# A hybrid encoder layer on one core: rare code moved beside the common code, the last additions shared out anew, one weight load halved

## The reference

```python
h = LN(x) * (1 + scale1) + shift1                 # x: two requests of 256 tokens, 1024 wide
z = h @ w_in + b_in                               # u | v | p | gates
merged = sig(g_a) * (A @ w_branch_a) + sig(g_b) * (P @ w_branch_b)
x = LN(ALPHA * x + gate1 * (merged @ w_out)) * ln1_g + ln1_b
h = LN(x) * (1 + scale2) + shift2
f = moe(h)     # top group of 4, top 2 of its 8 experts; each expert:
               # (silu(xb @ w_gate[e]) * (xb @ w_up[e])) @ w_down[e], width 1024 -> 512 -> 1024
y = LN(ALPHA * x + gate2 * f) * ln2_g + ln2_b
```

## Time and profile before

| | us |
|---|---|
| median of 3 runs | 978.49 |
| lowest, highest | 976.83, 981.91 |
| the profiled execution | 981.18 |
| its span, first to last instruction | 979.5 |
| TensorE busy in it | 912.4 (93%) |
| VectorE, ScalarE, GpSimd busy | 390.6, 242.7, 120.6 |

### The profile page before, as it was taken

How to read it: one execution, slowest core, us unless ns; L and a number is a source line. 1 busy time by engine, 2 the same in 40 slices (tenths; PEclk the granted TensorE clock), 3 DMA queues, 4 the chain that set the end, 5 groups by cost and what they waited for, 6 DMA issues and landing times.

```text
span 979.5 us, 11400 instructions
## 1 busy us (share of the span) xinstructions
PE 912.4 (93%) x4251; PEld 538.5 (55%) x4251; DVE 390.6 (40%) x664; ACT 242.7 (25%) x355; POOL 120.6 (12%) x144
## 2 busy tenths in 40 slices
PE   3789999999999999999999999999896999999973
PEld 1457776888888888786344434444443444344321
DVE  4522344456354236788332223222321222232265
ACT  2422243451234325445411101110110111011114
POOL 2110257000001000000300000000000000000041
PEclk9799999999999999999999999999998999999997
DMA  9884653362224623809899999999999599999953
GB/s 368 334 272 171 251 215 129 128 247 101 87 87 129 194 86 114 272 8 418 323 414 428 425 425 431 425 428 424 429 426 423 220 424 428 425 429 427 422 243 89
DMA packets 44860, 286.92 MB, mean 293 GB/s; under 512 B 5248, under 2 KB 7424, under 8 KB 29170
## 3 DMA queue, kind: packets, MB, share of 16 engines
q1 hardware_dynamic: 37504, 268.18, 67.6%
q0 software_dynamic: 6672, 16.17, 5.5%
q10 hardware_dynamic: 610, 1.66, 0.5%
HBM read 275.84 MB, written 14.58 MB: 297 GB/s over the span
## 4 chain that ended last, share of the span: by engine, by line
PE 83%; DVE 4%; ACT 3%; issue 3%; DMA 2%; SPq 2%; POOLq 0%; POOL 0%; DVEq 0%; ACTq 0%
PE bank L611 81%; DMA modraw<-in_w_mod 2%; PE bank L881 2%; SPq L389 2%; ACT x_rows L1086 2%; DVE total L1970 1%; DVE wo_lo L1650 0%; DVE yout L1858 0%; PE bank L668 0%; POOLq L53 0%; POOL y_out L605 0%; ACT w_hi L1086 0%; PE bank L897 0%; DVE yout L1856 0%; DVE bank L2073 0%
## 5 line engine op out<-in xcount | busy, mean ns | idle before, releaser
L611 PE MATMUL bank<-up_w,x_t 128*64 128x512 f32 x512 | 225.0, 592 | 0.0
L611 PE MATMUL bank<-gate_w,x_t 128*64 128x512 f32 x512 | 225.0, 592 | 0.0
L611 PEld LDWEIGHTS bank<-gate_w,x_t 128*64 128x64 f32 x512 | 70.1, 137 | 143.1 <-issue 143.1
L611 PE MATMUL bank<-h_hi,w_hi 128*128 128x512 f32 x320 | 126.3, 395 | 1.6 <-ACT h_hi L1120 1.6
L611 PE MATMUL bank<-h_hi,w_lo 128*128 128x512 f32 x320 | 125.9, 393 | 0.0
L611 PE MATMUL bank<-h_lo,w_hi 128*128 128x512 f32 x320 | 124.8, 398 | 0.0
L611 PE MATMUL bank<-down_w,hid_t 128*64 128x512 f32 x512 | 118.8, 606 | 6.0 <-issue 5.6
L1319 ACT ACTIVATE sg_hid<-bank 64x512 f32<-64x512 f32 x33 | 19.6, 592 | 348.9 <-PE bank L611 348.9
L1925 DVE TENSOR_TENSOR sg_hid<-bank,sg_hid 64x512 f32<-64x512 f32 x32 | 22.2, 695 | 207.2 <-ACT sg_hid L1319 207.2
L1485 DVE TENSOR_TENSOR w_lo<-raw,w_hi 128x1024 fp32r<-128x1024 f32 x56 | 68.6, 1227 | 78.3 <-ACT w_hi L1086 78.2
L568 POOL DMA_INDIRECT chosen_y<-yout,slot_row x30 | 29.5, 984 | 400.7 <-DVE yout L1943 400.7
(11 more groups left out here) (311 smaller groups left out, 1117.3 us busy)
## 6 DMA issues: line engine op xcount, KB each, us to landing
down_w<-in_w_exp_down SPq DMA_DIRECT2D x32, 2048.0 KB, 17.1
gate_w<-in_w_exp_gate SPq DMA_DIRECT2D x31, 2048.0 KB, 13.6
up_w<-in_w_exp_up SPq DMA_DIRECT2D x31, 2048.0 KB, 18.1
modraw<-in_w_mod SPq DMA_DIRECT2D x24, 1024.0 KB, 8.6
raw<-in_w_in SPq DMA_DIRECT2D x9, 2048.0 KB, 9.9
raw<-in_w_branch_b SPq DMA_DIRECT2D x2, 2048.0 KB, 12.2
chosen_y<-zrow POOLq DMA_DIRECT2D x1, 4096.0 KB, 16.6
raw<-in_w_branch_a SPq DMA_DIRECT2D x2, 2048.0 KB, 10.6
```

Of the source, the lines that this page charges most:

```text
L611: return pe.matmul(out, lhsT, rhs, start=start, stop=stop, skip_group_check=True)
```

## The change

The further code of ScalarE and VectorE is put beside the plain code: `joined_again` is given `with_further(e)` and makes its block before the common continuation. TensorE's stays where it is. At the end the final reads go tile by tile from 0, with a semaphore of its own for the second read of tile 0. VectorE does residual and second choices of tiles 0 and 1 and the residual of tile 2, all ahead of `out_rows(31)`, and gate rows and the first residual ahead of `hidden(31)`. GpSimd adds the second choices of tile 2 after all these, then those of tile 3, to which TensorE adds the residual by a further identity product. Tile 1 is stored through GpSimd's queue, and `gain(1)` comes before `centred_gain(3)`. Expert 3's gate and up weights are loaded in two parts, each of four transfers, the first when the first half of expert 0's gate product is done (`gum_half`); TensorE's wait counts for `e_gu[0]` and `e_half` are raised to match. TensorE has two more products with the identity, of 256 columns, in the router. ScalarE has a silu of one column ahead of its residual copy.

```diff
@@ -184,6 +184,7 @@
         slotw_x = at("slotw_x", [128, 1, 2], f32, V0 + 480)
+        silu_first = at("silu_first", [128, 1], f32, P0 + 64)
         slot_row_x = at("slot_row_x", [128, 1], u32, P0 + 32)
@@ -227,6 +228,7 @@
         s_out = sem("s_out")
+        s_out1 = sem("s_out1")
@@ -304,6 +306,8 @@
         f_g = [sem(f"f_g{i}") for i in range(TILES)]
+        f_second0 = sem("f_second0")
+        gum_half = sem("gum_half")
@@ -328,8 +332,12 @@
-        def joined_again(engine, name):
+        def joined_again(engine, name, further=None):
             engine.br(name + "_on")
+            if further is not None:
+                with nc.body(name + "_further", parent=parted_at[name], valid_engines=[engine.engine]):
+                    further()
+                    engine.br(name + "_on")
             nc.switch_bb(name + "_on", parent=parted_at[name])
@@ -436,7 +444,18 @@
             for e in range(3, NEXP - 2):
-                next_gate_up(e, e % 3)
+                if e == 3:
+                    done = sp.value_load(tab[0:1, 1, 1:2], min_val=0, max_val=16)
+                    for first, freed, loaded in ((0, gum_half, e_half), (2, m_sem["gum"], e_gu[0])):
+                        sp.wait_ge(freed, 1)
+                        sp.sem_inc(sp_go, 1)
+                        sp.wait_ge(x_sem["gum"], done + 1)
+                        sp.sem_inc(sp_go, 1)
+                        for tile, w in ((gate_w[0], w_exp_gate), (up_w[0], w_exp_up)):
+                            for k in (first, first + 4):
+                                sp.dma_start(tile[:, k:k + 2, :], gate_src(w, 3)[:, k:k + 2, :]).then_inc(loaded, 16)
+                else:
+                    next_gate_up(e, e % 3)
                 next_down(e - 1, (e - 1) % 2)
@@ -448,17 +467,17 @@
             sp.sem_inc(sp_go, 1)
-            for i in (2, 3, 0, 1):
-                for j, rows in enumerate((total[i], y_out[i])):
-                    sp.dma_start(rows[:, :], chosen_y[TOK * j + 128 * i:TOK * j + 128 * i + 128, :]).then_inc(f_g[i], 16)
-            for i, written, count in ((0, pool_f, 1), (2, f_o, 2), (1, pool_f, 2)):
+            for i in range(TILES):
+                sp.dma_start(total[i][:, :], chosen_y[128 * i:128 * i + 128, :]).then_inc(f_g[i], 16)
+                sp.dma_start(y_out[i][:, :], chosen_y[TOK + 128 * i:TOK + 128 * i + 128, :]).then_inc(f_g[i] if i else f_second0, 16)
+            for i, written, count in ((0, pool_f, 1), (2, f_o, 2)):
                 sp.wait_ge(written, count)
...
             sp.dma_start(y_prompt[0, HALF * last:HALF * last + HALF, :], y_out[last][0:HALF, :]).then_inc(s_out, 16)
-            sp.wait_ge(s_out, 32 * TILES)
+            sp.wait_ge(s_out, 32 * (TILES - 1))
@@ -596,13 +615,18 @@
                 expert(e)
-            for n, i in enumerate((2, 3, 0, 1)):
-                pool.wait_ge(f_g[i], 32)
-                pool.tensor_tensor(total[i][:, :], total[i][:, :], y_out[i][:, :], ALU.add).then_inc(pool_j, 1)
+            pool.wait_ge(f_b, 5)
+            pool.tensor_tensor(total[2][:, :], total[2][:, :], y_out[2][:, :], ALU.add).then_inc(pool_j, 1)
+            pool.wait_ge(f_g[3], 32)
+            pool.tensor_tensor(total[3][:, :], total[3][:, :], y_out[3][:, :], ALU.add).then_inc(pool_j, 1)
             pool.wait_ge(s_ln2, 32)
...
                 pool.tensor_tensor(y_out[i][:, :], y_out[i][:, :], ln2_bc[:, 1, :], ALU.add).then_inc(pool_f, 1)
+            pool.wait_ge(pool_f, 2)
+            for r, y in enumerate((y_prompt, y_sample)):
+                pool.dma_start(y[0, HALF:2 * HALF, :], y_out[1][HALF * r:HALF * r + HALF, :]).then_inc(s_out1, 16)
+            pool.wait_ge(s_out1, 32)
@@ -838,6 +862,7 @@
             keep_clock(1)
+            mm(B[7][:, 0:256], ident, cst[:, 0:256])
             pe.wait_ge(dve_rt, 1)
@@ -881,13 +906,15 @@
-            def gate_up(xt, s, bank, sm, halves=None, order=range(KC)):
+            def gate_up(xt, s, bank, sm, halves=None, order=range(KC), half_done=None):
...
                     x = mm(bank[CAP:128, :], xt[:, kc // 4, kc % 4, :], up_w[s][:, kc, :], start=(n == 0), stop=(n == KC - 1))
+                    if half_done is not None and n == KC // 2 - 1:
+                        x.then_inc(half_done, 1)
                 x.then_inc(sm["gum"], 1)
@@ -943,16 +970,18 @@
                 s, a = e % 3, e % 2
-                loaded = 32 * (e // 3 + 1)
+                loaded = 32 * (e // 3 + 1) + (32 if s == 0 and e >= 3 else 0)
                 if e:
                     more = pe.value_load(tab[0:1, 0, bass.ds(e, 1)], min_val=0, max_val=7)
+                if e == 3:
+                    pe.wait_ge(e_half, 64)
                 if last:
-                    pe.wait_ge(e_half, 32)
+                    pe.wait_ge(e_half, 96)
                 else:
...
                     pe.wait_ge(m_sem["xt"], 1)
-                    gate_up(x_t[:, 0:2, :, :], s, B[0], m_sem, halves=(m_sem["xt"], 2), order=(0, 1, 4, 5, 2, 3, 6, 7))
+                    gate_up(x_t[:, 0:2, :, :], s, B[0], m_sem, halves=(m_sem["xt"], 2), order=(0, 1, 4, 5, 2, 3, 6, 7), half_done=gum_half)
                 else:
@@ -1050,6 +1079,7 @@
             pe.wait_ge(act_h2, TILES)
+            mm(B[0][:, 0:256], ident, cst[:, 0:256])
             pe.wait_ge(m_sem["sl"], 1)
@@ -1065,13 +1095,19 @@
             near_rows(1, 1).then_inc(f_z, 1)
-            for i in (2, 3):
-                pe.wait_ge(f_b, i - 1)
+            def added(i, source, start=False):
                 for c in range(2):
-                    mm(sums[i][c][:, :], ident, total[i][:, 512 * c:512 * c + 512], start=(i == 3), stop=False)
-                if i == 3:
-                    near_rows(0, 3, start=False)
-                near_rows(1, i).then_inc(f_z, 1)
+                    mm(sums[i][c][:, :], ident, source[:, 512 * c:512 * c + 512], start=start, stop=False)
+
+            pe.wait_ge(pool_j, 1)
+            added(2, total[2])
+            near_rows(1, 2).then_inc(f_z, 1)
+            near_rows(0, 3)
+            pe.wait_ge(act_res, 1)
+            added(3, res[:, 3, :])
+            pe.wait_ge(pool_j, 2)
+            added(3, total[3])
+            near_rows(1, 3).then_inc(f_z, 1)
             pe.br("pe_end")
@@ -1312,6 +1348,7 @@
+            act.activation(silu_first[:, :], eps_col[:, :], ACT.Silu)
             copy(res[:, :, :], res[:, :, :], scale=ALPHA).then_inc(act_res, 1)
@@ -1371,7 +1408,7 @@
                 if e >= 2:
-                    joined_again(act, f"act_{e}")
+                    joined_again(act, f"act_{e}", lambda: with_further(e))
                 if e == 0:
@@ -1420,12 +1457,6 @@
             act.dma_start(y_sample[0, HALF * last:HALF * last + HALF, :], y_out[last][HALF:128, :]).then_inc(s_out, 16)
-            act.br("act_end")
-            for e in range(2, NEXP):
-                with nc.body(f"act_{e}_further", parent=parted_at[f"act_{e}"], valid_engines=[act.engine]):
-                    with_further(e)
-                    act.br(f"act_{e}_on")
-            nc.switch_bb("act_end")
@@ -1960,14 +1991,22 @@
                 if e == NEXP - 1:
-                    for n, i in enumerate((2, 3, 0)):
-                        with_residual(n, i)
-
-            def with_residual(n, i):
-                if n == 0:
-                    dve.wait_ge(act_res, 1)
-                dve.wait_ge(pool_j, n + 1)
+                    with_residual(0)
+                    with_second(0)
+                    with_residual(1)
+                    with_second(1)
+                    with_residual(2)
+
+            def with_residual(i):
+                dve.wait_ge(act_res, 1)
+                dve.wait_ge(f_g[i], 32 if i else 16)
                 dve.tensor_tensor(total[i][:, :], total[i][:, :], res[:, i, :], ALU.add).then_inc(f_b, 1)
+
+            def with_second(i):
+                if i == 0:
+                    dve.wait_ge(f_second0, 16)
+                dve.wait_ge(f_b, 2 * i + 1)
+                dve.tensor_tensor(total[i][:, :], total[i][:, :], y_out[i][:, :], ALU.add).then_inc(f_b, 1)
@@ -2005,14 +2044,20 @@
                     parted(dve, f"dve_{e}", more)
-                    hidden(e)
-                    gate_rows(e)
-                    next_chunks(e)
                     if e == NEXP - 1:
-                        for n, i in enumerate((2, 3, 0)):
-                            with_residual(n, i)
+                        gate_rows(e)
+                        with_residual(0)
+                        hidden(e)
+                        with_second(0)
+                        with_residual(1)
+                        with_second(1)
+                        with_residual(2)
+                    else:
+                        hidden(e)
+                        gate_rows(e)
+                        next_chunks(e)
                     out_rows(e)
-                    joined_again(dve, f"dve_{e}")
+                    joined_again(dve, f"dve_{e}", lambda: with_further(e))
                 if e < 2:
@@ -2029,7 +2074,7 @@
```

(11 more changed lines are left out.)

## The result

| | before | after |
|---|---|---|
| median us, runs side by side on one chip | 978.94 (5 runs, 976.83 to 981.91) | 983.95 (5 runs, 983.26 to 985.02) |
| ratio to before, 95% interval | | 1.0048, 1.0027 to 1.0069 |
| the profiled execution, its span | 981.18, 979.5 | 985.02, 983.3 |

The change made the kernel slower by 5.0 us; 15.0 less was forecast. First the shares of the chain by engine, of the page of after. DMA holds 5% of the chain where it held 2; by the page's lines the three points more are one each of a final read, a store of rows and the scatter of the slot table, through which the chain now runs. Waits for weights stand under issue, 4% for 3.

What follows compares the result with a forecast made beforehand. TensorE holds 83% of the span, so gains were sought in its gaps and behind its last product. Savings of 0.65, 0.8, 0.3, 3.85, 7.6 and 1.8 sum to 15.0: 978.5 becomes 963.5 us, range 959.5 to 970.

Steps and rivals of the forecast that it cites:

- silu and warm-up: Router: table load off expert 0's path saves about 0.65 us, warm-up products keeping the clock up save 0.8.
- weights in two parts: Expert 3's weight loads: an earlier first half moves the weights forward hardly more than the router's gain; 0.3 us saved.
- further round: Round at 742 to 762: both VectorE stalls go, TensorE's own branch then bounds the start; 3.85 us saved.
- running past the further code: Every other expert: VectorE and ScalarE jump over further code, any stall hidden by following idle time; cost 0.
- the end, stores by SyncE: After expert 31's down product: its multiplication starts 6.7 us earlier, 7.6 saved; last store issued earlier, 1.8 saved.
- stores by GpSimd: Tile 1's two stores through GpSimd's queue: the second lands at 976.1, about when tile 3's last one does.
- R1: Every expert: jumping further code costs VectorE 11.0 us against 6.5 of cover; about 1008 us, chance 0.04.
- the weights' lead afterwards is unhurt: After the round: full buffers set the lead, and the 14 us DMA pause at 0.24 only shrinks by 3.85.
- the gap of 3.6 us is still long enough for the clock to fall: TensorE at the round: the slow selection is kept, 6.04 us for the first 16 products.
- R2: End: tile 0's reads come 2 to 3 us later, VectorE holds the hidden product back; 966.5 to 969.5, chance 0.17.
- I take 1.8, bounds 0 and 2: Final stores: SyncE's last store goes with ScalarE's half of tile 3, 1.8 us earlier.
- R5: End: gains eaten by GpSimd's stores or a late addition; about 975 to 979 us, chance 0.04.

Runs made afterwards that it cites:

- e7: Kernel before with only the silu of one column and the two warm-up products: 980.4 us, ratio 0.9984 to the kernel before.
- e2: Kernel before with only expert 3's gate and up weights loaded in two parts: 981.77 us beside 981.3, ratio 1.0004.
- e11: Kernel before with eight satisfied waits in VectorE's far code of expert 2, which never runs, moving the code behind by four instructions: 974.8 us, ratio 0.9941.
- e6: Changed kernel with VectorE's and ScalarE's further-round code left at the end of their programs: 971.99 us, ratio 0.9908 to the kernel before.
- e4: Kernel before with only the new end, tile 1 stored by SyncE as before: 967.8 us, ratio 0.9864.
- e3: Kernel before with only the new end, tile 1 stored by GpSimd, which waits for its stores: 973.94 us, ratio 0.9925.
- e1_beside: Kernel before with only VectorE's and ScalarE's further-round code put beside the expert's own: 984.61 us, ratio 1.0026.
- e8: Kernel before with VectorE's further-round code beside the expert's own, ScalarE's still at the end: 984.77 us, ratio 1.0038.
- e9: Kernel before with silu, warm-up products and the new end with SyncE's stores; further-round code far, expert 3's weights whole: 964.79 us, ratio 0.9835.
- e12: e1_beside with forty satisfied waits (twenty instructions) more in each further-round piece of VectorE and ScalarE: 988.28 us, ratio 1.0073 to the kernel before.
- e15: e11 with a hundred satisfied waits in VectorE's plain code of each expert from 2 on: 990.67 us, ratio 1.0098 to the kernel before.
- e13: e11 with sixty-four satisfied waits in VectorE's plain code of each expert from 2 on: 981.75 us, ratio 1.0020 to the kernel before.
- e5: Changed kernel, but SyncE instead of GpSimd waits for the landing of tile 1's stores: 980.23 us, ratio 0.9992 to the kernel before.

## Why the prediction was wrong

| term (us saved) | predicted | measured by |
|---|---|---|
| silu and warm-up | 1.45 | 1.6 (-0.6 to 3.6), e7 |
| weights in two parts | 0.3 | -0.4 (-2.1 to 1.3), e2 |
| further round | 3.85 | 5.8, e11 |
| running past the further code | 0 | -13.7, after against e6 |
| the end, stores by SyncE | 9.4 | 7.5, e4 less e11 |
| stores by GpSimd | in the 9.4 | -6.0, e3 against e4 |
| sum | 15.0 | -5.2 (measured -5.0) |

The measured column comes from ratios of different runs, and that its sum fits to 0.2 us is partly luck: the intervals are about 2 us either way for e7, e2 and e11, and roughly 3 for each difference of two runs. The parts are also not free of one another. The 13.7 us hold what the lag did to the new end, where the late read holds back the hidden product; in the kernel with the old end the placement cost 8.3 (e1_beside less e11_shift, 1.0026 less 0.9941).

**The step that failed.** "Each such jump is followed by idle time ... I cost it at nothing." As far as it goes that is right: no expert's hidden product waits for a branch in after, and R1, which looked for the price on VectorE itself, was wrong too. But the cover was sought on the engine alone. Code is a transfer: VectorE ran through more of it, nine more blocks of 8 KB came, and one of the sixteen DMA engines, which are full there (a share of 1.01 from 520 to 740), landed its part of each weight load up to 5.7 us late. TensorE starts a down product when the last part is there. I had costed the DMA's side of this edit only at the pause ("the weights' lead afterwards is unhurt"), not ahead of it.

The Trainium skill ("Runtime: NRT & Kernel Launch", section on instruction fetch mechanics), which the prediction cites for the stalls, also says that each sequencer fetches through a DMA queue of its own and that crossing a block is "mostly hidden". Fetches do stand in the trace as packets of queues of instructions, but it doesn't show one queue for each engine: q14's count rises with ScalarE's code (39 for 37) as with VectorE's (44). With "mostly hidden" it agrees only on the engine itself: hidden from VectorE, paid at the weights, 13.7 us. The section's block is 16 KiB; the packets of q14 have 8 KB.

That all data of a transfer has landed only when the full 16 have counted, and that the up to sixteen engines it runs on finish independently, is told by the Trainium skill too ("DMA: Bandwidth & Descriptors", section on why a DMA increments its semaphore by 16). The landings here agree, with 5.2 us between the last two of the load that the product of 729.6 waited for.

**The further round.** "VectorE's branch ... then reaches code right behind the plain one; both stalls go" was right, and TensorE's branch became the bound as forecast (3.19 us of gap for 3.6). But the step took both stalls as the price of distance. Four instructions of padding take the second away at no cost and leave the first hidden behind TensorE's own branch. Nothing was left for the placement to win. The clock at the round stayed up in e11 (3.92 us for the 16 products), which I had not counted, so 5.8 and not 3.85. I had written that the gap of 3.6 us is still long enough for the clock to fall; behind gaps of the same size it fell in some kernels (6.73 us for the products in e6 behind 3.44, 5.51 in after behind 3.19) and stayed up in others (3.92 in e11 behind 3.42, in e8 behind 3.04). These runs don't say what decides it.

**The end.** The reorder did what was forecast where the reads came in time (e4: the multiplication starts 0.1 us behind the down product, no gap, full clock). In after the reads came 4 us late, and what the prediction named as R2 happened ("VectorE holds the hidden product back"), by 3.4 us, with the lag as its reason: the read's sixteenth part came 3.5 us behind the others. R2 had 0.17 as a case by itself; it came with the lag and on top of it.

**The stores.** "I take 1.8, bounds 0 and 2" failed. The step ended with the landing of the last store and did not ask what stands behind it. The closing rows of before show it (the drain ends at 979.3, of a span of 979.5). R5 named GpSimd's stores with 0.04 and 975 to 979; the mechanism was real, at 6.0 us, but alone it would not have made the kernel slower.

**Router and split.** Both within what was forecast. The first selection took 3.67 us for 5.21, and the silu's table load (466.26) left the path; of some 2.4 us there, 1.6 may reach the end. The split moved loads into the pause of the slot table and won nothing.

The range (959.5 to 970) missed because all cases in it took the placement as a gain of 0 to 7.4; the only one against it looked at a single engine.

**What stays open.** How a fetch of 8 KB, whose packets take 0.3 us each, makes an engine fall behind by some 0.7 us per expert (from 0.5 us at 588 to 5.3 at 698 in after) was not shown; nor which DMA engine it is, since the trace doesn't name it. That e9 lags by 3.3 us with 33 fetches shows that their number isn't all. That VectorE's code beside makes the lag rests on e8 and e6; that its amount does, and not the jump, on e12 and on the lag of e15. e13 alone would have left it undecided, and the time of e15 doesn't measure what the lag costs. That it is one and the same DMA engine each time is read from one part of sixteen being late in load after load.

## What to carry to other kernels

Where the DMA engines are full, code is traffic: rare code that the common path has to run past costs fetches on every pass, and one late DMA engine makes every load late, so leave it far, and look first whether a far branch stalls twice: moving the code by a few instructions may take one stall away. Here it was VectorE's code that cost; ScalarE's alone, with two fetches more, changed nothing that could be measured. Follow an end to the last row of the last engine: a store or a wait on GpSimd puts its closing drain behind everything. Ahead of a product on the path, put no addition whose operand comes by a transfer with less than a few microseconds to spare.

## What the runs showed of the hardware

- GpSimd's closing drain took 6.53 us behind a wait (after, e3_end, e6), some 6.4 behind an addition (8.77 less 2.35: before, e4, e7, e9) and 8.2 behind stores still open (e5). The other engines' took at most 3.2 us (TensorE in e6).
- Moving code by four instructions that never run was worth 5.8 us. A far branch of VectorE was followed by 5.4 to 6.1 us of stall (longest piece behind the branch in twelve kernels), and by 5.0 to 5.1 more in the kernels whose far code stood where before's does.
- Satisfied waits were paired, two to an instruction of 50 ns, mostly one every 0.1 us (e13, e15).
